# Four POOL subtractions of 512 columns in place of one of 2048, in a two-block transformer kernel

## The chip, the cores and the metric

The kernel runs on one core of a Trainium2 chip. Its time is the device time of one execution in microseconds (us). Five engines work side by side, each through its own queue of instructions, and are tied together by semaphores: PE (TensorE, matrix products), DVE (VectorE), ACT (ScalarE), POOL (GpSimd) and SP (SyncE, which here issues nearly all transfers).

## The reference

The input is 256 tokens of width 1024. The reference runs two blocks, one after the other. Cut to what matters here:

```
first_block:   adaptive RMS norm, convolution branch + attention branch, mixture of 32 experts (top 4), RMS norm
second_block:  x = layer_norm_2(x)
  layer 0:     mix = hybrid_mixer(x)           # attention + retention, gates
               x = layer_norm_2(ALPHA*x + mix)
               x = layer_norm_2(ALPHA*x + (silu(x @ w1) * (x @ w3)) @ w2)       # dense, width 2816
  layer 1:     mix = hybrid_mixer(x)
               x = layer_norm_2(ALPHA*x + mix)
               x = layer_norm_2(ALPHA*x + mixture of 8 experts (top 2))

layer_norm_2:  mu = mean(x); var = mean((x - mu)^2); (x - mu) * rsqrt(var + eps) * g + b
```

All of it is float32. Each weight matrix is read once from memory in pieces of 1 MB (128 partitions by 2048 columns).

## The kernel before, in words

The activations stand transposed, features on the partitions and tokens along the columns, as `X` (eight tiles of 128 features by 256 tokens; a "pair" is two of these, 512 columns).

For some of the second block's products (the projections qa, kva, ret and gg of both mixers, and ffn1 and ffn3 of the dense layer) the kernel doesn't multiply in float32. It writes weight and activation each as a sum of two parts in the faster type fp32r, a high part and a low part, and makes three passes: high weight by high x, low weight by high x, high weight by low x. There are 60 such pieces of weight, q = 0 to 59 in this profile's rows (19 of mixer 0, 22 of the dense layer, 19 of mixer 1). `split_dense` makes the two parts of piece q: ACT copies the raw weight into `WHI_D` (L379, which rounds it), then POOL subtracts that from the raw weight and writes `WLO_D` (L382). Both have room for four pieces. PE waits in `split_ready` for the low part of piece q, so for POOL; a raw slot is given back to SP for the next transfer by the same semaphore, `dense_lo`; and ACT may overwrite high part q only when PE has finished piece q - 4 (`lin_done`).

Nothing else orders POOL's work but its program: the pieces follow each other in the order of q; in the mixers two short masks of the retention decay (L565, L567) stand between a piece and the next. ACT splits as its own order allows: pieces 0 to 3 of each of the three stretches are split ahead, while a layer norm is still being computed, the others one by one as PE finishes pieces.

The layer norms before these stretches are what the prediction looks at. In each, DVE first takes a cheap estimate of the mean (SHIFT, L1650) from the columns. Then for each of four pairs it subtracts it (L2065 in the first norm, L2097 and L2100 in the others) and squares the result (`squared`, L1653). PE adds each pair and its squares over the partitions by products with a matrix of ones (`moments`, L727), for which it waits for DVE's square. In the first norm PE adds one more set of squares (L1000) between the third and the last pair. Then follow mean, variance and root on DVE and ACT (L1659 on), and the first product of the next stretch (`first_jobs`, L662). In the two later norms (after the mixer's w_out and after the dense layer) the pairs are mixed into the last products of the layer: L641 and L1235 are those products on PE, L2085 and L2201 DVE's adding of their results out of PSUM.

All of L2065, L2097, L2100 and L1653 read two operands from SBUF. L2085 and L2201 read one from SBUF and one from PSUM.

Of the kernel before, what the change touches and what calls it, by code (L numbers as in the profile page):

```python
# [20 lines left out]
F32 = mybir.dt.float32  # L21
F32R = mybir.dt.float32r
I32 = mybir.dt.int32
ALU = mybir.AluOpType
# [23 lines left out]
SLOT = 2048  # L48
# [90 lines left out]
def build_two_blocks(nc, A, out):  # L139
# [3 lines left out]
    with ctx:  # L143
        sems = {}

        def sem(name):
            if name not in sems:
                sems[name] = ctx.enter_context(nc.semaphore(name))
            return sems[name]
# [52 lines left out]
        def slot(n):  # L202
            r = n % RING if n < N_A else (n - N_A) % RING2
            return W[:, r * SLOT:(r + 1) * SLOT], r
# [162 lines left out]
        def split_dense(eng, q):  # L367

            n, _ = split_slots[q]
            raw, r = slot(n)
            if q >= SPLIT_N:
                eng.wait_ge(sem("lin_done"), split_slots[q - SPLIT_N][1])
            hi, lo = WHI_D[:, q % SPLIT_N, :], WLO_D[:, q % SPLIT_N, :]
            if eng is nc.scalar:
                eng.wait_ge(sem(f"arrived{r}"), arrive[n][1])
                eng.activation(hi, raw, ACT.Copy).then_inc(sem("dense_hi"), 1)  # L379
            else:  # L380
                eng.wait_ge(sem("dense_hi"), q + 1)
                eng.tensor_tensor(lo, raw, hi.bitcast(F32), ALU.subtract).then_inc(sem("dense_lo"), 1)  # L382

        def ring1(s):

# [127 lines left out]
        def _(pool):  # L513
# [42 lines left out]
            def mixer2(l):  # L556
                q0 = 41 * l
                for q in range(q0, q0 + 11):
                    split_dense(pool, q)
                for h in range(HEADS):  # L560
                    n = l * HEADS + h
                    pool.wait_ge(sem("decay_exp"), n + 1)
                    dec = DEC[:, h % 2, :]

                    ch.link(pool.affine_select(out=dec[:, 0:P], in_=dec[:, 0:P], compare_op=ALU.is_ge, fill=0.0,  # L565
                                               base=0, pattern=[[1, P]], channel_multiplier=-1))
                    pool.affine_select(out=dec[:, 3 * P:], in_=dec[:, 3 * P:], compare_op=ALU.is_gt, fill=0.0,  # L567
                                       base=0, pattern=[[-1, P]], channel_multiplier=1)\
                        .then_inc(sem("decay_masked"), 1)
                    split_dense(pool, q0 + 11 + h)  # L570

                pool.wait_ge(sem("ret_weighted"), HEADS * (l + 1))
                ch.link(pool.memset(SPREAD, 0.0))
                spread = SPREAD.rearrange("p k (g c) -> p k g c", g=2)
                for half in range(2):
                    i = pool.affine_select(out=spread[:, :, half, :], in_=spread[:, :, half, :], compare_op=ALU.not_equal,
                                           fill=1.0, base=-half, pattern=[[-2, KT], [0, HD]], channel_multiplier=1)
                i.then_inc(sem("pool_tables"), 1)
# [8 lines left out]
            for q in range(19, 41):  # L587
                split_dense(pool, q)
# [1671 lines left out]
```

## Time and profile before

| | |
|---|---|
| median of three runs | 2513.7 us (2511.43 to 2516.62) |
| the profiled execution's own time | 2516.26 us |
| its span, first to last instruction | 2514.5 us |
| PE busy | 2351.5 us, 94% |
| DVE busy | 724.7 us, 29% |
| ACT busy | 587.0 us, 23% |
| POOL busy | 298.9 us, 12% |
| mean granted TensorE clock | 0.966 |

A time of the table is that of a whole execution; the rows further down give the start of an instruction or a group of them in us from the start of the span, and how long it took. Busy time of DVE and POOL contains any time in which an instruction has been started and can't go on. The granted clock is a share of 2.4 GHz: 1.00 is that level, 0.50 is 1.2 GHz.

### The profile page before, as it was taken

Reading aid. Unit: us, or ns where it says so; the run is one execution under the profiler, and the core shown is the slowest. Engines: PE = TensorE matmul, PEld = TensorE weight load, DVE = VectorE, ACT = ScalarE, POOL = GpSimd, SP = SyncE. Lnnn points to the kernel's source line nnn. Section 1 sums busy time; section 2 is a strip of 40 time slices with the busy share of each in tenths; the row PEclk is TensorE's granted clock in tenths of the full one; section 3 lists DMA queues with packets and bytes.
Section 4 is the critical chain, followed back from the end, with each engine's and each line's share of the span. In section 5 each row is a group of like instructions: output and inputs, shape, how many; then the busy total and the mean of one; then the engine's idle time right before and its main releaser. Section 6 shows DMA issues by size and latency. Waiting matters only on the chain.

```text
span 2514.5 us, 35242 instructions
## 1 busy us (share of the span) xinstructions
PE 2351.5 (94%) x13516; PEld 1499.8 (60%) x13517; DVE 724.7 (29%) x1360; ACT 587.0 (23%) x865; POOL 298.9 (12%) x129
## 2 busy tenths in 40 slices
PE   3999879999999999999988999999899979999997
PEld 2887744444444444444447887899798874445444
DVE  5854222232222222222243324100313341111113
ACT  1033011121121111121233741430257011111111
POOL 1000000000000000000005532580265000000000
PEclk9999979999999999999998999999999979999998
DMA  9952449999999999989973423553543357799751
GB/s 374 363 176 86 117 166 417 418 418 417 418 418 418 418 418 417 417 339 418 418 306 116 135 68 117 168 185 117 168 137 107 110 225 276 290 407 402 278 231 62
DMA packets 226327, 688.60 MB, mean 274 GB/s; under 512 B 31338, under 2 KB 120242, under 8 KB 190418
## 3 DMA queue, kind: packets, MB, share of 16 engines
q1 hardware_dynamic: 221776, 685.82, 71.1%
q10 hardware_dynamic: 4482, 1.81, 0.3%
q8 instruction: 50, 0.82, 0.1%
q14 instruction: 19, 0.16, 0.0%
HBM read 686.53 MB, written 1.05 MB: 273 GB/s over the span
## 4 chain that ended last, share of the span: by engine, by line
PE 71%; DMA 11%; SPq 10%; DVE 5%; issue 2%; ACT 1%; ACTq 1%; DVEq 0%
PE PS L939 15%; PE PS L630 11%; PE PS L641 11%; DMA RAW<-in_w_exp_in 9%; SPq L434 6%; PE PS L1050 6%; PE PS L903 4%; PE PS L1061 3%; PE PS L1235 3%; SPq L456 2%; PE PS L922 2%; PE PS L1014 1%; PE PS L685 1%; PE PS L727 1%; PE PS L662 1%
## 5 line engine op out<-in xcount | busy, mean ns | idle before, releaser
L939 PE MATMUL PS<-RAW,Z 128*64 128x512 f32 x3168 | 715.5, 598 | 24.4 <-DMA RAW<-in_w_exp_in 23.6
L939 PEld LDWEIGHTS PS<-RAW,Z 128*64 128x64 f32 x3168 | 214.3, 137 | 456.3 <-issue 377.8
L382 POOL TENSOR_TENSOR WLO_D<-W,WHI_D 128x2048 fp32r<-128x2048 f32 x60 | 275.9, 4603 | 1321.7 <-ACT WHI_D L379 1321.7
L1050 PE MATMUL PS<-W,Z 128*64 128x384 f32 (+1 forms) x1408 | 216.0, 464 | 7.0 <-DMA W<-in_moe_w 5.8
L641 PE MATMUL PS<-Z,W 128*128 128x256 f32 x768 | 174.2, 388 | 2.2 <-DVE Z L1815 1.5
L1050 PEld LDWEIGHTS PS<-W,Z 128*64 128x64 f32 x1408 | 99.9, 138 | 124.2 <-issue 66.7
L641 PEld LDWEIGHTS PS<-Z,W 128*128 128x128 f32 x768 | 149.4, 195 | 26.0 <-DVE Z L1815 1.9
L379 ACT ACTIVATE WHI_D<-W 128x2048 fp32r<-128x2048 f32 x60 | 114.4, 1906 | 167.6 <-DMA W<-in_w_in 92.5
L903 PE MATMUL PS<-Z 128*128 128x64 f32 x1088 | 128.6, 278 | 3.1 <-DVE Z L1922 3.1
L903 PEld LDWEIGHTS PS<-Z 128*128 128x128 f32 x1088 | 127.4, 196 | 3.8 <-DVE Z L1907 3.8
L641 PE MATMUL PS<-H,W 128*128 128x256 f32 x512 | 118.3, 393 | 5.7 <-DVE H L1641 4.7
L1938 DVE TENSOR_TENSOR Z<-Z,PS 128x1024 f32<-128x1024 f32 x66 | 80.4, 1218 | 125.9 <-PE PS L922 125.9
L641 PEld LDWEIGHTS PS<-H,W 128*128 128x128 f32 x512 | 100.0, 197 | 21.3 <-DVE H L1641 4.8
L630 PE MATMUL PS<-XHI,WHI_D 128*128 128x256 f32 x784 | 112.0, 285 | 0.0
L630 PE MATMUL PS<-XHI,WLO_D 128*128 128x256 f32 x784 | 110.0, 283 | 0.0
L630 PE MATMUL PS<-XLO,WHI_D 128*128 128x256 f32 x784 | 110.0, 283 | 0.0
L1061 PE MATMUL PS<-W,Z 128*64 128x512 f32 x484 | 108.7, 597 | 0.0
L1450 ACT ACTIVATE Z<-PS 128x512 f32<-128x512 f32 x33 | 19.7, 597 | 367.6 <-PE PS L939 367.6
L630 PEld LDWEIGHTS PS<-XHI,WHI_D 128*128 128x128 f32 x784 | 100.6, 191 | 7.2 <-issue 7.2
L1965 DVE COPY Z<-PS 128x512 f32<-128x512 f32 x33 | 22.8, 692 | 280.5 <-PE PS L939 280.5
L630 PEld LDWEIGHTS PS<-XLO,WHI_D 128*128 128x128 f32 x784 | 101.1, 192 | 0.0
L630 PEld LDWEIGHTS PS<-XHI,WLO_D 128*128 128x128 f32 x784 | 101.1, 192 | 0.0
(376 smaller groups left out, 2410.6 us busy)
## 6 DMA issues: line engine op xcount, KB each, us to landing
RAW<-in_w_exp_in SPq DMA_DIRECT2D x256, 1024.0 KB, 19.3
RAW<-in_w_exp_out SPq DMA_DIRECT2D x128, 1024.0 KB, 21.8
W<-in_moe_w SPq DMA_DIRECT2D x128, 704.0 KB, 15.1
W<-in_w_in SPq DMA_DIRECT2D x52, 1024.0 KB, 5.7
W<-in_moe_w SPq DMA_DIRECT2D x40, 1024.0 KB, 14.4
W<-in_ffn_w SPq DMA_DIRECT2D x33, 1024.0 KB, 5.2
W<-in_w_ada SPq DMA_DIRECT2D x24, 1024.0 KB, 13.8
W<-in_w_out SPq DMA_DIRECT2D x12, 1024.0 KB, 4.9
```

Source lines behind the costliest of these rows:

```text
L379: eng.activation(hi, raw, ACT.Copy).then_inc(sem("dense_hi"), 1)
L382: eng.tensor_tensor(lo, raw, hi.bitcast(F32), ALU.subtract).then_inc(sem("dense_lo"), 1)
L434: sp.dma_start(dst, src).then_inc(sem(f"raw{s}"), 16)
L456: sp.dma_start(first2(s)[:, 1408 * i:1408 * (i + 1)], w[0, bass.ds(e, 1), s * P:(s + 1) * P, :].rearrange("a p n -> p (a n)"))\
L630: mm = pe.matmul(ps(job % 2, T, c0=j * T), w[:, k, c:c + P], xp[:, k, :], start=(i == k == 0), stop=(i == 2 and k == KT - 1))
L641: mm = pe.matmul(ps(job % 2, T, c0=j * T), w[:, k, c:c + P], x[:, k, :], start=(k == 0), stop=(k == nk - 1))
L903: mm = pe.matmul(ps(2, HALF, c0=k * HALF), HT[:, a, k * P:(k + 1) * P], PICK[:, a, 0:HALF], start=(a == 0), stop=(a == 1))
L939: mm = pe.matmul(ps(bank, 512, 64 * h, 64 * h + 64), x, w[:, c:c + 512], start=first, stop=final, skip_group_check=True)
L1050: mm = pe.matmul(ps(2 * i + b, n, 64 * h, 64 * h + 64), X1[:, s, :], first2(s)[:, c:c + n], start=(s == 0), stop=(s == 7), skip_group_chec ...
L1061: mm = pe.matmul(ps(2, 512, 64 * h, 64 * h + 64), x, second2(j)[:, c:c + 512], start=(i == j == 0), stop=(j == 5), skip_group_check=True)
L1235: mm = pe.matmul(ps(j // 2, T, c0=(j % 2) * T), w[:, i, j * P:(j + 1) * P], Z[:, k * T:(k + 1) * T], start=(k == 0 and j % 2 == 0), stop=( ...
L1938: dve.tensor_tensor(o, o, PS[:, 6:8, :].rearrange("p h (k t) -> p h k t", k=2), ALU.add)\
```

## The change

The low part of a piece is made by four POOL instructions of 512 columns in place of one of 2048. The bytes read and written are the same. The semaphore is raised by the fourth alone, so PE, ACT and SP are told at the same point of POOL's program as before. Nothing else is edited.

```
             else:
                 eng.wait_ge(sem("dense_hi"), q + 1)
-                eng.tensor_tensor(lo, raw, hi.bitcast(F32), ALU.subtract).then_inc(sem("dense_lo"), 1)
+                for c in range(0, SLOT, 512):
+                    i = eng.tensor_tensor(lo[:, c:c + 512], raw[:, c:c + 512], hi[:, c:c + 512].bitcast(F32), ALU.subtract)
+                i.then_inc(sem("dense_lo"), 1)
```

POOL's program where the second block begins, before. The iota of the first block is followed by pieces 0 to 10; the waits of each are given.

```order
L582 IOTA Z 128x256 [waits moe_scratch_free]
L382 TENSOR_TENSOR WLO_D<-W,WHI_D 128x2048 [waits dense_hi] x4
L382 TENSOR_TENSOR WLO_D<-W,WHI_D 128x2048 [waits dense_hi,lin_done] x7
L565 AFFINE_SELECT W<-W 128x128 [waits decay_exp]
L567 AFFINE_SELECT W<-W 128x128 [waits pool_step]
```

The same place now (pieces 0 and 1, then 4 and the masks; lines stand two or less further down the file):

```order
L584 IOTA Z 128x256 [waits moe_scratch_free]
L383 TENSOR_TENSOR WLO_D<-W,WHI_D 128x512 [waits dense_hi]
L383 TENSOR_TENSOR WLO_D<-W,WHI_D 128x512 x3
...
L383 TENSOR_TENSOR WLO_D<-W,WHI_D 128x512 [waits dense_hi,lin_done]
L383 TENSOR_TENSOR WLO_D<-W,WHI_D 128x512 x3
L567 AFFINE_SELECT W<-W 128x128 [waits decay_exp]
L569 AFFINE_SELECT W<-W 128x128 [waits pool_step]
```

The order of pieces and masks is kept. Within a piece the first instruction waits and the three behind it wait for nothing.

The second place is where POOL leaves mixer 0 for the dense layer, before (the spread table of the retention norm, then pieces 19 to 51):

```order
L573 MEMSET W 16x1024 [waits ret_weighted]
L576 AFFINE_SELECT W<-W 16x8x64 [waits pool_step]
L576 AFFINE_SELECT W<-W 16x8x64
L382 TENSOR_TENSOR WLO_D<-W,WHI_D 128x2048 [waits dense_hi,lin_done] x33
L565 AFFINE_SELECT W<-W 128x128 [waits decay_exp]
```

And now (the two last rows stand 33 times):

```order
L575 MEMSET W 16x1024 [waits ret_weighted]
L578 AFFINE_SELECT W<-W 16x8x64 [waits pool_step]
L578 AFFINE_SELECT W<-W 16x8x64
L383 TENSOR_TENSOR WLO_D<-W,WHI_D 128x512 [waits dense_hi,lin_done]
L383 TENSOR_TENSOR WLO_D<-W,WHI_D 128x512 x3
```

33 instructions became 132 there; over the program 60 became 240. The other engines' programs are the same as before.

## Rows read from the trace of the kernel before

**Rows 1.** The page's costliest groups: busy us, mean ns, idle before and releaser.
```profile
L382 POOL TENSOR_TENSOR WLO_D<-W,WHI_D 128x2048 fp32r<-128x2048 f32 x60 | 275.9, 4603 | 1321.7 <-ACT WHI_D L379 1321.7
```

**Rows 2.** PE's waits in the whole program: us in total, times, longest.
```profile
PE PS L727 <- DVE H L1653: 10.0, 4, 4.7
```

**Rows 3.** Timeline of DVE, first norm: start us, us, instruction.
```profile
1316.87 2.37 DVE L2065 TENSOR_TENSOR Z<-Z,SQ 128x512 f32<-128x512 f32 x1
1319.28 4.94 DVE L1653 TENSOR_TENSOR Z<-Z 128x512 f32<-128x512 f32 x1
1324.14 4.98 DVE L2065 TENSOR_TENSOR Z<-Z,SQ 128x512 f32<-128x512 f32 x1
1329.16 0.69 DVE L1653 TENSOR_TENSOR Z<-Z 128x512 f32<-128x512 f32 x1
```

**Rows 4.** Timeline of POOL, first norm (pieces 0, 1 and 2).
```profile
1314.17 4.52 POOL L382 TENSOR_TENSOR WLO_D<-W,WHI_D 128x2048 fp32r<-128x2048 f32 x1 [1007.05 <-ACT WHI_D L379]
1319.15 9.42 POOL L382 TENSOR_TENSOR WLO_D<-W,WHI_D 128x2048 fp32r<-128x2048 f32 x2 [0.47 <-ACT WHI_D L379]
```

**Rows 5.** Timeline of PE, first norm.
```profile
1324.27 3.78 PE L727 MATMUL PS<-Z,ONES 128*128 128x256 f32 x8 [7.90 <-DVE Z L1653]
1329.91 6.77 PE L727 MATMUL PS<-Z,ONES 128*128 128x256 f32 x16 [1.85 <-DVE Z L1653]
1336.51 3.62 PE L1000 MATMUL PS<-H,ONES 128*128 128x256 f32 x16
```

**Rows 6.** Windows: length, busy PE, PEld, DVE, ACT, POOL, granted clock, DMA, GB/s.
```profile
1329.90:1336.50 6.60, 6.59 (x16) 5.30 (x17) 2.54 (x4) 0.00 (x0) 0.00 (x0) 0.53 0.48 155
```

**Rows 7.** Timeline of DVE, second norm (after w_out of mixer 0).
```profile
1556.93 4.29 DVE L2097 TENSOR_TENSOR X<-X,SQ 128x512 f32<-128x512 f32 x1
...
1561.87 6.32 DVE L2100 SCALAR_TENSOR_TENSOR X<-X,SQ 128x512 f32<-128x512 f32 x3
```

**Rows 8.** Timeline of POOL, second and third norm (pieces 20, 21, 43, 44).
```profile
1556.15 4.52 POOL L382 TENSOR_TENSOR WLO_D<-W,WHI_D 128x2048 fp32r<-128x2048 f32 x1 [2.54 <-ACT WHI_D L379]
1563.09 4.55 POOL L382 TENSOR_TENSOR WLO_D<-W,WHI_D 128x2048 fp32r<-128x2048 f32 x1 [2.41 <-ACT WHI_D L379]
...
1789.73 4.52 POOL L382 TENSOR_TENSOR WLO_D<-W,WHI_D 128x2048 fp32r<-128x2048 f32 x1 [1.14 <-ACT WHI_D L379]
1798.35 5.03 POOL L382 TENSOR_TENSOR WLO_D<-W,WHI_D 128x2048 fp32r<-128x2048 f32 x1 [4.10 <-ACT WHI_D L379]
```

**Rows 9.** Timeline of PE, second norm.
```profile
1556.20 7.07 PE L641 MATMUL PS<-Z,W 128*128 128x256 f32 x32
...
1569.69 2.07 PE L727 MATMUL PS<-X,ONES 128*128 128x256 f32 x4 [4.69 <-DVE H L1653]
...
1573.26 7.96 PE L641 MATMUL PS<-Z,W 128*128 128x256 f32 x32
```

**Rows 10.** Timeline of DVE, third norm (after the dense layer).
```profile
1792.38 2.41 DVE L2097 TENSOR_TENSOR X<-X,SQ 128x512 f32<-128x512 f32 x1
...
1799.65 4.28 DVE L1653 TENSOR_TENSOR H<-X 128x512 f32<-128x512 f32 x1
```

**Rows 11.** Timeline of PE, third norm (third pair and fourth pair).
```profile
1803.99 2.07 PE L727 MATMUL PS<-X,ONES 128*128 128x256 f32 x4 [2.92 <-DVE H L1653]
...
1807.36 1.03 PE L727 MATMUL PS<-X,ONES 128*128 128x256 f32 x4
```

**Rows 12.** POOL's shortest kind of instruction: one column.
```profile
L540 POOL IOTA IOTAP<- 128x1 f32 x1 | 0.1, 137 | 0.1
```

**Rows 13.** Timeline of POOL: pieces 23 to 26, and 40, the dense layer's last.
```profile
1604.57 18.39 POOL L382 TENSOR_TENSOR WLO_D<-W,WHI_D 128x2048 fp32r<-128x2048 f32 x4 [29.06 <-ACT WHI_D L379]
...
1698.16 4.62 POOL L382 TENSOR_TENSOR WLO_D<-W,WHI_D 128x2048 fp32r<-128x2048 f32 x1 [1.13 <-ACT WHI_D L379]
```

**Rows 14.** Timeline of PE: first matrix products of pieces 23 and 40.
```profile
1615.27 1.12 PE L630 MATMUL PS<-XHI,WHI_D 128*128 128x256 f32 x8
...
1713.19 1.12 PE L630 MATMUL PS<-XHI,WHI_D 128*128 128x256 f32 x8
```

## The prediction, made before the changed kernel had run

> **What bounds the kernel now.** I read the page first: PE is busy 94% of the span, POOL 12%, in 60 instructions of 4.60 us each [rows 1]. By that POOL is no bound, and a change of its instructions could be worth nothing. The next view is who waits for whom, PE alone: it never waits for POOL. But it waits 10.0 us in four places for a square that DVE makes in the layer norms [rows 2], and in the first norm 7.90 and 1.85 us more [rows 5]. Third I read DVE's timeline at these waits, and that is where the change comes in. A subtraction or square of 512 columns takes DVE 0.69 us, yet three in a row end after 2.37, 4.94 and 4.98 us [rows 3]. POOL's timeline says why: its pieces run from 1314.17 to 1318.69 and, two of them, from 1319.15 to 1328.57 [rows 4]. The first long DVE instruction ends at 1319.24, 0.55 after POOL's piece; the third ends at 1329.12, again 0.55 after the end of a piece. In the second norm L2097 ends at 1561.22, and the piece at 1560.67: 0.55 [rows 7, 8]. In the third L1653 ends at 1803.93, the piece at 1803.38: 0.55 [rows 8, 10]. So a DVE instruction with both operands in SBUF stands still until the POOL instruction that runs has ended, and then needs 0.55 us. It holds the other way round as well: piece 44, begun at 1798.35 beside such a DVE instruction, takes 5.03 in place of 4.52 us [rows 8].
>
> The Trainium skill says the same ("SBUF — State Buffer", section on the two separate sides): a DVE instruction with two SBUF inputs and a GpSimd instruction that reads SBUF lock each other out for a whole instruction and don't share bandwidth. The trace agrees, by the four ends 0.55 us apart. Were it a sharing of bandwidth, cutting the instruction would bring nothing.
>
> Fourth I asked whether DVE gets its turn between two POOL instructions when POOL has the next one at hand. The middle of [rows 4] is the one case: pieces 1 and 2 take 9.42 us together, and within that L1653 ends at 1324.22 [rows 3], 0.55 after 1323.67, where piece 1 must have ended. Piece 2 then needs 4.35 us more (1328.57 less 1324.22). So they take turns.
>
> **What four short instructions cost on POOL.** No row shows such an instruction. From below: 4.52/4 = 1.13 us. From above: a POOL instruction for a single column takes 0.14 us [rows 12]; taken as pure start-up and added to 4.60/4 it makes 1.29. I take 1.20, between them. A piece is then 4.8 us (4.5 to 5.2) in place of 4.6.
>
> The Trainium skill gives figures for this operation ("GPSIMD Engine Reference", section on elementwise work): 2.6 cycles per element at 1.2 GHz and 4497 ns for 2048 columns. That leaves 60 ns for start-up and would make 1.17 us each, an estimate from that page; the sum would be the same. No run shows the split yet.
>
> Does this price reach PE? PE takes a new piece each 5.76 us in the dense layer ((1713.19 - 1615.27)/17 [rows 14]), POOL is through with piece 40 at 1702.78 [rows 13] and PE wants it at 1713.19: 10.4 us of cover, and POOL keeps up as long as a piece takes under 5.76 us. In the mixers the cadence is no faster. So 0 us, and still 0 at 1.29.
>
> **What it gives on DVE.** Turns: after a POOL instruction DVE needs 0.55 us; the next POOL instruction then needs its own time less 0.17 (4.52 less 4.35), so 1.03. A turn costs 1.58 us (1.51 to 1.67) where it was 4.90. I go through the three norms with that.
>
> *First norm.* DVE asks at 1316.87. POOL's quarters end at 1315.37, 1316.57, 1317.77, so DVE's first ends at 1318.3 and the following at steps of 1.58: the second (pair one ready) at 1319.9, the fourth (pair two) 1323.1, the sixth (pair three) 1326.2, the eighth 1329.4. POOL has work all along, since seven quarters do and twelve are to be made. PE starts pair one at 1319.9 and not at 1324.27 [rows 5]. Its products go at the lower level there, granted clock 0.53 from 1329.9 to 1336.5 [rows 6], 0.42 us each (6.77/16), 3.4 us a pair. So PE ends pair one at 1323.3, two at 1326.7, three at 1330.1, nearly without a gap, where before it idled between pairs. L1000 then starts at 1330.1 in place of 1336.51: 6.4 us. If the clock comes back one pair earlier (L1000's products take 0.22 us at the full level: 3.62/16), pair three takes 1.7 and it is 8.1 us. The worst: the clock stays low to the end of L1000 and the last pair; 24 products at 0.42 in place of 0.22 cost 4.8 us, and 1.6 are left. I take 7.0 (1.6 to 8.1).
>
> *Second norm.* DVE asks at 1556.93, the first quarter of piece 20 ends at 1557.35, and DVE's five instructions end at 1557.9, 1559.5, 1561.1, 1562.6 and, since piece 21 comes only at 1563.09, 1563.3. L2085 reads PSUM: 1564.0. The square of the next pair waits for one quarter and ends about 1565.0; PE has worked until then (the products of the first pair end about 1564.9) and does not wait 4.69 us [rows 9]. What follows ran at a lower clock after that wait: four products 2.07 us and the next 32 in 7.96 us, where the same take 1.03 and 7.07 [rows 9], and the other four of the pair cost about 0.9 more as well: 2.8 us. Full gain 7.5. If one more turn comes in the way, 1.6 less. If three turns do and the clock falls all the same, 2.5 are left. I take 6.0 (2.5 to 7.5).
>
> *Third norm.* The wait of 2.92 us [rows 11] and the slow products behind it (1803.99 to 1807.36 for eight that take 1.73 at full clock: 1.6 more). DVE's first instruction there, 2.41 us long, waits for piece 43 and was hardly on the path. Its second, which ran free, may meet the last quarter. With quarters DVE has pair three ready near 1800.5 in place of 1803.93; PE comes to it at 1800.6 and to the fourth pair at 1802.4 instead of 1807.36. That is 5.0; if pair two, which ran free before piece 44, now meets a quarter, 3.8. Only the wait shortened by two thirds and the clock still low: 1.9. I take 4.2 (1.9 to 5.0).
>
> Sum: 7.0 + 6.0 + 4.2 = 17.2 us (ends 6.0 and 20.6). The second mixer's last norm has no splits beside it, so nothing. In the mixers' attention DVE's 512-column instructions read PSUM and are not held. A gain in these norms moves everything behind it: PE works without such waits from each norm to the next, and the transfers there are issued as PE frees slots. The profiled execution took 2516.3 us, its span and 1.8 around it, so 2499.1 by its own time; it lies 2.6 above the median of the runs. Against the median, 2513.7 - 17.2 = 2496.5.
>
> **The rivals.**
> *No turn between quarters.* The three behind the first wait for no semaphore. POOL's queue may have them all under way before DVE asks, and DVE waits for four as it did for one. For it: pieces 23 to 26 ran in 18.39 us, 4.60 each, without a gap [rows 13], so POOL starts the next at once. Against it: pieces 1 and 2 also followed each other with the high part long made, and DVE came between. The semaphore wait between them is what is missing now. Time: gain 0, five long waits each longer by up to 0.3 us, 2514 to 2515. The Trainium skill's rule in "SBUF — State Buffer", on who interferes with whom, is that the order of issue decides who blocks; it doesn't say who is first between two queued instructions. Chance 0.11.
>
> *Turns, but PE's clock doesn't follow.* DVE's waits shrink but with one or two turns more than I count, and PE's products stay as slow as before. For it: after a wait of 2.92 us the clock fell, so one of 2 us could do it too. Gain about 4.4 (pair one earlier in the first norm) + 2.5 + 1.9 = 8.8, so 2504.9. Chance 0.30.
>
> *POOL becomes the bound.* If a quarter had a start-up far above 0.14 us, POOL would fall behind. Piece 23 starts at 1604.57 and PE wants piece 40 at 1713.19 [rows 13, 14], 18 pieces in 108.6 us: from 6.03 us a piece, 1.51 a quarter, PE waits in the dense layer, 18 x (c - 6.03). To lose the 17.2 us there c must be 7.0, a quarter 1.75 us; at 2.0 us a quarter it is 35 less 17, so 18 slower: 2532. Against it: 1.75 would be 0.6 of start-up where the shortest POOL instruction as a whole takes 0.14. Chance 0.03.
>
> *It doesn't do what it says.* No: 240 instructions of 512 columns stand in the program.
>
> **How the numbers follow.** The forecast of 2496.5 has 0.56, with its own range 2492 to 2501. Two in ten left out: the range goes from 2491 up to 2508, past the second rival. This kernel's runs differ by 0.1 to 0.2%, so 0.2%, 5 us, is about what can be told from no change. Faster by that: the forecast and nearly all of the second rival, 0.85. Within: the first rival and the rest, 0.12. Slower: 0.03.
>
> **What the profile after would show.** POOL's group: x240 at 1.13 to 1.29 us. DVE's L2065, L1653, L2097 and L2100: no instruction over about 1.8 us. PE's wait before the first L727 about 3.5 us and not 7.9; L1000 starts 14 to 16 us after POOL's first piece in place of 22; no wait of 4.7 us in the second norm. Behind the norms the timelines only shift. The forecast is wrong if DVE instructions of over 4 us remain (first rival), if they are short but L727 still comes at 0.42 to 0.47 us a product after the waits (second), or if PE waits for WLO_D at all (third).

## The result, and the profile after

The changed kernel takes 2493.6 us (median of four runs, 2493.1 to 2494.3) where the kernel before takes 2513.4 us (median of four): a ratio of 0.9924, interval 0.9911 to 0.9938. 19.7 us were gained; 17.2 were forecast. The profiled execution took 2493.8 us, with a span of 2492.1.

I read the views in the order of the prediction. POOL's group on the page, to be compared with [rows 1]:

```profile
L383 POOL TENSOR_TENSOR WLO_D<-W,WHI_D 128x512 fp32r<-128x512 f32 x240 | 308.8, 1322 | 1277.8 <-ACT WHI_D L379 1277.8
```

The same work keeps POOL busy for 33 us longer. The mean of 1322 ns is a little over the 1.29 us that the prediction gave as the upper end: a quarter that shares its time with DVE shows up to 1.76 us, and one that follows another starts 0.03 to 0.05 us before the end of the one ahead. From start to start, undisturbed quarters are 1.22 to 1.27 us apart. Then PE's waits for a square of DVE, which were 10.0 us for `H` [rows 2] and 9.75 for `Z` [rows 5]:

```profile
PE PS L729 <- DVE H L1655: 4.8, 3, 2.0
...
PE PS L729 <- DVE Z L1655: 3.7, 2, 2.9
```

So 11.3 us of PE's waiting went, and yet 19.7 us were gained. The timelines show where the rest came from. First norm, DVE (start, duration, instruction), against [rows 3]:

```profile
1313.49 0.69 DVE L2067 TENSOR_TENSOR Z<-Z,SQ 128x512 f32<-128x512 f32 x1
1314.22 1.65 DVE L1655 TENSOR_TENSOR Z<-Z 128x512 f32<-128x512 f32 x1
1315.79 1.76 DVE L2067 TENSOR_TENSOR Z<-Z,SQ 128x512 f32<-128x512 f32 x1
1317.59 1.64 DVE L1655 TENSOR_TENSOR Z<-Z 128x512 f32<-128x512 f32 x1
```

POOL beside it, pieces 0 to 2 in twelve instructions, against [rows 4]:

```profile
1311.10 18.40 POOL L383 TENSOR_TENSOR WLO_D<-W,WHI_D 128x512 fp32r<-128x512 f32 x12 [1006.94 <-ACT WHI_D L379]
```

And PE, against [rows 5]:

```profile
1315.92 5.96 PE L729 MATMUL PS<-Z,ONES 128*128 128x256 f32 x16 [2.92 <-DVE Z L1655]
1322.63 1.99 PE L729 MATMUL PS<-Z,ONES 128*128 128x256 f32 x8 [0.74 <-DVE Z L1655]
1324.46 3.62 PE L1002 MATMUL PS<-H,ONES 128*128 128x256 f32 x16
```

DVE's ends are 1.68 us apart (1317.55 to 1319.23). That is the turn: one POOL instruction, one DVE instruction. The first L2067 took 0.69 us, since a quarter ended (at 1313.61) just after DVE had asked. PE's first wait is 2.92 and not 7.90 us, and 16 products take 5.96 us where they took 6.77, the last eight 1.99. The windows of the same stretch say why (length, busy PE, PEld, DVE, ACT, POOL, granted clock, DMA, GB/s):

```profile
1315.90:1319.30 3.40, 3.38 (x8) 2.55 (x9) 3.37 (x3) 3.40 (x6) 3.40 (x3) 0.50 0.31 68
1319.30:1321.80 2.50, 2.50 (x9) 1.91 (x8) 2.47 (x2) 0.59 (x1) 2.50 (x2) 0.76 0.95 334
```

The clock leaves 1.2 GHz during the second pair; in [rows 6] it was still at 0.53 in the third. PE is then ahead of DVE: it waits 0.74 us for the third square. L1002 starts 11.4 us after DVE's first step of the norm (L1652 at 1313.04). Before it was 20.1. After POOL's first piece it starts 13.4 us (1324.46 less 1311.10), where the prediction looked for 14 to 16.

Second norm, DVE, against [rows 7], and PE, against [rows 9]:

```profile
1544.84 0.95 DVE L2099 TENSOR_TENSOR X<-X,SQ 128x512 f32<-128x512 f32 x1
1545.82 1.64 DVE L1655 TENSOR_TENSOR H<-X 128x512 f32<-128x512 f32 x1
1547.38 5.24 DVE L2102 SCALAR_TENSOR_TENSOR X<-X,SQ 128x512 f32<-128x512 f32 x3
```
```profile
1554.35 1.13 PE L729 MATMUL PS<-X,ONES 128*128 128x256 f32 x4 [1.45 <-DVE H L1655]
...
1556.18 7.07 PE L643 MATMUL PS<-Z,W 128*128 128x256 f32 x32
```

The wait is 1.45 in place of 4.69 us, and the products behind it run at full clock: 1.13 in place of 2.07 and 7.07 in place of 7.96. Third norm, DVE and PE, against [rows 10, 11]:

```profile
1780.16 1.41 DVE L1655 TENSOR_TENSOR H<-X 128x512 f32<-128x512 f32 x1
...
1782.20 1.05 DVE L1655 TENSOR_TENSOR H<-X 128x512 f32<-128x512 f32 x1
```
```profile
1781.62 1.13 PE L729 MATMUL PS<-X,ONES 128*128 128x256 f32 x4 [1.33 <-DVE H L1655]
```

The wait has moved: the second pair's square, free before, now meets a quarter (1.41), and the third pair's no longer stands for 4.28 (1.05).

Of the prediction's other signs, no DVE instruction of the four lines takes over 1.77 us, and PE never waits for a low part.

For all runs I cut the span at the same places. "Norm" is from the start of SHIFT on DVE (first norm) or of its sum on PE (second, third) to the first product of `first_jobs`; what lies between is "mixer 0", "dense", "mixer 1". Worked out from the timelines, us:

| run | norm 1 | mixer 0 | norm 2 | dense | norm 3 | mixer 1 |
|---|---|---|---|---|---|---|
| before | 30.82 | 208.11 | 34.19 | 201.26 | 23.32 | 206.05 |
| four of 512 (the change) | 22.14 | 208.06 | 28.33 | 200.79 | 19.57 | 205.86 |
| e1: all but the norms' pieces in four | 29.67 | 206.75 | 34.23 | 201.18 | 23.22 | 206.05 |
| e2: two of 1024 | 27.62 | 205.86 | 28.43 | 200.51 | 22.89 | 206.49 |
| e3: eight of 256 | 21.14 | 208.18 | 26.61 | 200.12 | 19.55 | 207.94 |
| e4: sixteen of 128 | 27.09 | 214.44 | 30.82 | 213.03 | 24.30 | 215.04 |
| e5: nine pieces, eight of 256 | 20.95 | 208.06 | 26.60 | 200.06 | 18.94 | 206.51 |
| e6: nine pieces, sixteen of 128 | 27.03 | 206.27 | 30.32 | 201.24 | 24.31 | 208.00 |
| e7: as e6, linked | 20.47 | 208.25 | 26.61 | 200.86 | 18.11 | 208.31 |
| e8: whole, five held | 22.78 | 206.60 | 26.61 | 199.97 | 18.47 | 205.88 |
| e9: four of 512, PE filled | 22.14 | 204.98 | 28.33 | 199.66 | 19.53 | 205.70 |
| e10: whole, PE filled in norm 2 | 30.64 | 208.09 | 31.33 | 201.00 | 23.08 | 205.97 |
| e11: pieces 0 to 2 in four | 22.15 | 207.96 | 33.93 | 201.28 | 23.26 | 206.12 |
| e12: e8 with PE filled | 21.42 | 205.52 | 26.61 | 199.67 | 18.50 | 205.66 |

The norms gained 8.68 + 5.86 + 3.75 = 18.3 us, the stretches between them 0.7. The spans differ by 22.4; the other 3.4 lie ahead of the first norm, which the profiled execution of before reached at 1316.41 and this one at 1313.04. 3.1 of them are there when POOL starts its first piece (1314.17 and 1311.10), so the change can't have made them. They are the spread between executions (the medians differ by 19.7), and differences up to about 2 us in the mixers are taken as such too: mixer 0 takes 206.27 us in e6, where its pieces are whole as before, against 208.11.

### The profile page after: what moved, and what is told of

It reads as the page before. It is cut to its first block, busy times and chain, and to the rows that moved or that the text cites. A ratio compares the mean times of both kernels' runs of the same rounds, so it can differ in the third digit from the quotient of the medians.

```text
span 2492.1 us, 35422 instructions
## 1 busy us (share of the span) xinstructions
PE 2343.3 (94%) x13516; PEld 1494.2 (60%) x13517; DVE 717.5 (29%) x1360; ACT 587.4 (24%) x865; POOL 331.8 (13%) x309
## 3 DMA queue, kind: packets, MB, share of 16 engines
HBM read 686.53 MB, written 1.05 MB: 276 GB/s over the span
## 4 chain that ended last, share of the span: by engine, by line
PE 74%; DMA 11%; SPq 8%; DVE 4%; issue 1%; ACT 1%; ACTq 1%; DVEq 0%
PE PS L941 16%; PE PS L632 11%; PE PS L643 11%; DMA RAW<-in_w_exp_in 9%; PE PS L1052 7%; SPq L436 6%; PE PS L1063 4%; PE PS L905 4%; PE PS L1237 3%; PE PS L924 2%; PE PS L1016 2%; PE PS L687 1%; PE PS L664 1%; PE PS L729 1%; PE PS L952 1%
## 5 line engine op out<-in xcount | busy, mean ns | idle before, releaser
L383 POOL TENSOR_TENSOR WLO_D<-W,WHI_D 128x512 fp32r<-128x512 f32 x240 | 308.8, 1322 | 1277.8 <-ACT WHI_D L379 1277.8
L1452 ACT ACTIVATE Z<-PS 128x512 f32<-128x512 f32 x33 | 19.7, 597 | 367.0 <-PE PS L941 367.0
```

The lines of the kernel that those rows point to most:

```text
L383: i = eng.tensor_tensor(lo[:, c:c + 512], raw[:, c:c + 512], hi[:, c:c + 512].bitcast(F32), ALU.subtract)
```

## The experiments

The theory: DVE instructions with both operands in SBUF and POOL's subtractions shut each other out for a whole instruction, a shorter instruction makes the wait shorter, and with it goes a time of low clock on PE. The rivals: the cut helps by itself wherever it is made; all is the wait, nothing the clock; POOL's start-up sets an end. Each ratio is to executions of the kernel before that were taken with the experiment (medians 2510.2 to 2510.7 us), so runs are compared by ratio.

**e1. Everything cut but the norms.**

```
+ w = SLOT if q in (0, 1, 2, 20, 21, 22, 42, 43, 44) else 512
```

> All pieces are cut into four except the nine that run beside a layer norm (0 to 2, 20 to 22, 42 to 44), which stay whole. Theory (turns between POOL and DVE in the three norms are the whole gain): no gain, 2512 to 2515 us; DVE's L2067, L1655 and L2102 again 4 to 5 us where they meet a piece. Rival (the cut helps by itself, in the 51 pieces beside the matrix products too): a good part of the 20 us stays, 2500 or less. POOL's group at 1.26 us for a cut instruction.

Ratio 1.0005 (0.9994 to 1.0016), 2513.4 us: no gain, and the interval leaves room for 1.5 us at most. PE's waits are those of before:

```profile
PE PS L730 <- DVE H L1656: 10.1, 4, 4.9
PE PS L730 <- DVE Z L1656: 10.1, 2, 8.2
```

204 of the 240 short instructions, beside the matrix products, are worth nothing that can be told. The gain lies in the nine pieces.

**e11. Only the first norm's pieces.** `w = 512 if q in (0, 1, 2) else SLOT`

> Only pieces 0, 1 and 2 cut into four, the rest whole. Theory (the norms' gains add up, each of its own): the first norm as with four everywhere, 22.1 us in place of 30.8, the second and third as before (34.2 and 23.3), gain 9 us, ratio 0.9965. Rival (an earlier start is given back in the next stretch, because transfers then pace it): a longer stretch between the norms, and a gain under 5.

Ratio 0.9966 (0.9952 to 0.9979), 8.5 us on 2511. Norm 1 takes 22.15 us as with all pieces cut, norms 2 and 3 stay near before, and the stretch behind is not longer. So the gain of this norm does not need the cuts in the others, and it is kept.

**e2. Two of 1024.** `w = 1024`

> Two instructions of 1024 columns for a piece. Theory: a DVE instruction waits for one POOL instruction, so a turn is the POOL instruction (2.33 us free) plus 0.44, 2.8 us, between the 4.9 of one and the 1.7 of four. First norm 3 us earlier (2 to 5), second 1, third 1.5: gain 5.5, 2508 us (2504 to 2510). Rival (the gain comes with any cut, since what matters is that POOL's queue lets DVE in at all): nearly the full 20 us, 2494 to 2497.

Ratio 0.9977 (0.9966 to 0.9988), 2505.2 us. DVE in the first norm:

```profile
1316.17 2.73 DVE L1656 TENSOR_TENSOR Z<-Z 128x512 f32<-128x512 f32 x1
1318.82 2.83 DVE L2068 TENSOR_TENSOR Z<-Z,SQ 128x512 f32<-128x512 f32 x1
```

A turn is 2.75 us (1318.90 to 1321.65), 2.8 expected. The price follows POOL's instruction, not the mere fact of a cut. By norms it came otherwise than I had split it: 3.2, 5.8 and 0.4, for 3, 1 and 1.5. Norm 2 turned on a near tie: DVE's third L2103 and the first half of piece 21 both start at 1554.05, and DVE gets through in 0.69 us. PE's wait is 1.55 us there and its clock stays up. The norms of this profile gained 9.4 us, more than the 5.8 of the ratio: the ten executions run from 2500.0 to 2507.7 us and the profiled one is the fastest of them, so such ties may fall otherwise in the rest. There is no profile of those.

**e3. Eight of 256.** `w = 256`

> Eight instructions of 256 columns. Start-up per further instruction 0.14 us ((4.94 - 4.52)/3), so 0.69 us each, 5.5 to 5.6 us a piece, under the 5.76 of PE's cadence: POOL still hidden. A turn is 0.70 + 0.44 = 1.14 us. Theory: the waits left in the norms (2.92, 1.45, 1.33 us) shrink by 1.1, 1.2 and 0.8, and 1 more in the first norm: gain 4 over four instructions, 2490 us (2488 to 2492). Rival (POOL's start-up grows faster, and PE waits for low parts): slower than four instructions, 2495 or more.

2492.1 us, ratio 0.9918 (0.9897 to 0.9938). 1.5 us better than four by the medians, within the intervals of both; 4 was expected. The norms gave 1.0, 1.7 and 0.0, and the second mixer took 2.1 more in this profile. PE's waits show no cause for it, so it counts as spread. The turn is 1.14 us as worked out. POOL stays hidden: 64 instructions in 44.53 us, 0.70 each, 5.6 a piece:

```profile
1344.71 44.53 POOL L384 TENSOR_TENSOR WLO_D<-W,WHI_D 128x256 fp32r<-128x256 f32 x64 [12.06 <-ACT WHI_D L379]
```

**e4. Sixteen of 128.** `w = 128`

> Sixteen instructions of 128 columns. By 0.14 us of start-up a piece is 4.6 + 15 x 0.14 = 6.7 us, over PE's 5.76: POOL sets the pace. PE waits for WLO_D in the dense layer, 18 x 6.7 - 108.6 = 12 us, and 1 us in each mixer; the finer turns give back 5. Theory: 2503 us (2498 to 2508), with PE waits on POOL in the profile. Rival (start-up is hidden in the instruction before, 0.08 or less each): a piece stays under 5.8, nothing is lost, 2488 to 2490.

2532.8 us, ratio 1.0083 (1.0064 to 1.0103): 21 to 22 us slower than before, not 7 faster. Three things are in it. POOL's pace is as worked out, 120.94 us for 288 instructions, 6.7 a piece, and the dense layer is 11.8 us longer, 12.1 by 18 x (6.7 - 6.03):

```profile
1599.69 120.94 POOL L384 TENSOR_TENSOR WLO_D<-W,WHI_D 128x128 fp32r<-128x128 f32 x288 [21.34 <-ACT WHI_D L379]
```

The mixers lose 6.3 and 9.0 us, not 1 each. I had left out the masks that stand behind the pieces in POOL's program; DVE gets them late in two places (its longest wait for L570, the second mask, is 5.3 us where it was 1.4) and PE waits for DVE. These waits of PE are 9.4 of the 15.3 us; for the rest PE's products ran longer (busy 1.0 and 5.9 us more). The waits, us in total, times, longest:

```profile
DVE W L2142 <- POOL W L570: 25.2, 16, 5.3
PE PS L1144 <- DVE W L2142: 9.4, 2, 5.6
PE PS L633 <- POOL WLO_D L384: 9.0, 13, 0.7
```

And the norms, in which finer turns should have given 5 us, lost two thirds of the gain (27.1, 30.8, 24.3 us: 6.1 of 18.3 are left). DVE in the first one, and POOL's batch beside it:

```profile
1313.47 0.69 DVE L2068 TENSOR_TENSOR Z<-Z,SQ 128x512 f32<-128x512 f32 x1
...
1318.39 0.94 DVE L2068 TENSOR_TENSOR Z<-Z,SQ 128x512 f32<-128x512 f32 x1
...
1327.88 6.97 DVE L1663 SCALAR_TENSOR_TENSOR SQ<-SQ 128x256 f32<-128x256 f32 x1
```
```profile
1311.07 23.50 POOL L384 TENSOR_TENSOR WLO_D<-W,WHI_D 128x128 fp32r<-128x128 f32 x48 [1007.05 <-ACT WHI_D L379]
```

The third row is the surprise of the study. At 1313.47 DVE comes to the running batch, behind six of its instructions, and gets its turn at once (0.69 us); as long as it then comes one instruction after the other, it keeps getting it (0.94 us). Eight us after the last of these it comes anew, and stands for 6.97 us until 1334.85; the batch had ended at 1334.57. When it came, POOL had put 18 instructions behind each other without DVE. In the other two norms it is the same: DVE stands for 5.3 and 5.7 us behind 23 and 20 such instructions. This is the prediction's first rival, no turn between short instructions, true in these places and not elsewhere in the same batches.

The runs with wider instructions do not settle whether the width decides or the number. The most that e3 had run undisturbed when DVE came, 12 instructions of 256 columns, took as long as e4's 20 (8.2 us), and DVE got in:

```profile
1763.35 12.95 POOL L384 TENSOR_TENSOR WLO_D<-W,WHI_D 128x256 fp32r<-128x256 f32 x16 [1.41 <-ACT WHI_D L379]
```
```profile
1771.55 0.76 DVE L2100 TENSOR_TENSOR X<-X,SQ 128x512 f32<-128x512 f32 x1
```

So it is not the time alone. 18 or more in a row were never met at 256.

**e6. Sixteen of 128, in the norms only.** So that POOL is not behind anywhere else.

```
+ w = 128 if q in (0, 1, 2, 20, 21, 22, 42, 43, 44) else SLOT
```

> The same nine pieces in sixteen of 128 columns. With all pieces cut so, three DVE instructions stood still for 5.3 to 7.0 us until POOL's whole batch had ended, beside others that got their turn after 0.2. Theory (POOL instructions this short leave DVE no opening when it comes new to a batch that is running): again DVE instructions of 4 us and more, and a gain of 10 to 16 us, smaller than with 256 columns. Rival (those three came from POOL being behind in the matrix stretches): no DVE instruction over 1.3 us, gain 22.

Ratio 0.9978 (0.9968 to 0.9987): 5.5 us of gain, less than the 10 to 16 that I gave the theory, but the DVE instructions are there, three again at the same places (7.10, 5.22, 5.68 us), behind the same 18, 23 and 20 undisturbed instructions. DVE in norms 1 and 2:

```profile
1327.48 7.10 DVE L1663 SCALAR_TENSOR_TENSOR SQ<-SQ 128x256 f32<-128x256 f32 x1
...
1565.14 5.22 DVE L1656 TENSOR_TENSOR H<-X 128x512 f32<-128x512 f32 x1
```

**e7. The same, each POOL instruction waiting for the one before.**

```
+                    if c + w < SLOT:
+                        cuts[0] += 1
+                        i.then_inc(sem("cut"), 1)
+                        eng.wait_ge(sem("cut"), cuts[0])
```

> As the run with nine pieces in sixteen of 128 columns, but each POOL instruction waits on a semaphore for the one before. If DVE is kept out because the next POOL instruction is already under way when one ends, it now always gets its turn: no DVE instruction over 1.3 us in the norms, at a price of 0.05 to 0.1 us per instruction on POOL, 1 to 1.5 us a piece, hidden. Gain 20 to 23 us. If the waits change nothing, DVE instructions of over 4 us are left as without them.

2489.9 us, ratio 0.9912 (0.9893 to 0.9931). The same two DVE instructions:

```profile
1326.66 0.42 DVE L1669 SCALAR_TENSOR_TENSOR SQ<-SQ 128x256 f32<-128x256 f32 x1
...
1559.63 0.98 DVE L1662 TENSOR_TENSOR H<-X 128x512 f32<-128x512 f32 x1
```

Same pieces, same columns, 16 us less: the shutting out needs POOL instructions that follow each other without a wait, for here DVE got in behind 14, 18 and 16 linked ones. The link also leaves POOL idle for about 0.08 us before each, and the run doesn't part that gap from the wait. The price of the link is 0.12 us, a little over the 0.05 to 0.1 expected: where DVE is away, linked instructions start 0.53 us apart (1320.05 to 1320.58) and unlinked ones 0.41. The first batch as a whole shows more, 0.66 each, since DVE's turns lie in it:

```profile
1309.93 25.77 POOL L386 TENSOR_TENSOR WLO_D<-W,WHI_D 128x128 fp32r<-128x128 f32 x39 [1006.52 <-ACT WHI_D L381]
```

A piece takes 8.5 us so (16 x 0.53), over 10 beside DVE's turns, which nine pieces can bear.

**e5. Eight of 256, in the norms only.** `w = 256 if q in (0, 1, 2, 20, 21, 22, 42, 43, 44) else SLOT`

> Only the nine pieces beside the norms are cut, into eight of 256 columns; the other 51 stay whole. Theory: the norms gain as with eight everywhere (first 9.7, second 7.6, third 3.8 us by the profiles), and the low parts beside matrix products are whole and early again: ratio to before about 0.9915, 21 us. Rival (cutting the other 51 also gives something): less than 17 us.

Ratio 0.9927 (0.9900 to 0.9954). One of its four executions took 4351 us and is left out of the ratio, which makes it a rough one. By the profile the norms gained 9.9, 7.6 and 4.4 us, 21.9 together, as expected; the ratio says 18 with 7 to either side, so the run agrees but adds little in the whole time.

**e8. No cut, five pieces held back.**

```
+                hold = {1: ("xw_shifted", 1), 2: ("normed", 8), 20: ("evac_dve", job_evac[lins["w_out0"].job0 + 2][1]),
+                        22: ("normed", 12), 44: ("normed", 16)}
+                if q in hold:
+                    eng.wait_ge(sem(hold[q][0]), hold[q][1])
```

> All pieces whole as before, but five are held back on POOL until DVE is past the part of a norm that they disturb: piece 1 until the last pair is shifted, 2, 22 and 44 until the norm is done, 20 until the third pair is added. Theory (the collision is all there is, not the length of an instruction): the waits of 7.9, 1.9, 4.7 and 2.9 us go without any cut; first norm 6 to 8.5 us, second 7, third 5, gain 18 to 20.5. Rival (held pieces come too late, and PE waits for WLO_D): a wait of PE on POOL in the profile, gain under 12.

2489.5 us, ratio 0.9908 (0.9888 to 0.9928), 21 to 23 us, a little more than expected. DVE's instructions in the second norm take 0.69 us, and POOL comes afterwards, released by DVE:

```profile
1545.21 0.69 DVE L2101 TENSOR_TENSOR X<-X,SQ 128x512 f32<-128x512 f32 x1
1545.93 0.69 DVE L1657 TENSOR_TENSOR H<-X 128x512 f32<-128x512 f32 x1
```
```profile
1552.44 9.42 POOL L386 TENSOR_TENSOR WLO_D<-W,WHI_D 128x2048 fp32r<-128x2048 f32 x2 [10.58 <-DVE X L2089]
```

PE waits for no low part. The length of the instruction was never the fault; the collision was. Norm 1 took 22.78 us, 0.64 more than in the changed kernel. Piece 0, still whole and not held, kept the first pair back: PE starts it 3.8 us after SHIFT, not 2.9. DVE had the second and third sooner, but PE could make no use of it, since its products ran at the low clock for longer (24 in 8.42 us):

```profile
1318.04 8.42 PE L731 MATMUL PS<-Z,ONES 128*128 128x256 f32 x24 [3.85 <-DVE Z L1657]
```

**e10. The clock's share, in norm 2.** The kernel before, with products of constants on PE during its wait.

```
                         moments(X, H, 0, True, False, 5, 4)
+                        for i in range(10 if l == 0 else 0):
+                            pe.matmul(ps(7, T), ONES[:, :], DIST[:, 0, :], start=True, stop=True)
                         moments(X, H, 1, False, False, 5, 4)
```

> The kernel before, POOL's pieces whole, with ten such products on PE between the first and the second pair of the second norm alone, where it waits 4.69 us for DVE. DVE comes no earlier. Theory (2.6 of the 5.9 us won in that norm are the clock, 3.2 the wait): from the first sum of that norm to the next first product 31.6 us in place of 34.2, with the products of the second pair at 0.22 us each. Rival (all of it is the wait): 34.2 as before. In the whole time 2.6 us are hardly to be told.

Norm 2 takes 31.33 us, 2.9 less, with DVE as late as ever. PE:

```profile
1560.77 4.48 PE L1219 MATMUL PS<-DIST,ONES 128*128 128x256 f32 x20
1565.40 1.13 PE L727 MATMUL PS<-X,ONES 128*128 128x256 f32 x4
```

The four products after the wait take 1.13 and not 2.07 us. So about half of what the change won in this norm (5.86) was clock. (The whole time, ratio 0.998 with 0.9971 to 0.9989, holds a gain of 2.9 us, at its lower end.)

**e9. The same filling ahead of first_jobs, on the changed kernel.**

```
 def first_jobs(lin):
+    for i in range(10):
+        pe.matmul(ps(7, T), ONES[:, :], DIST[:, 0, :], start=True, stop=True)
```

> The four-instruction kernel with ten further products (of constants, into a PSUM bank that nothing else uses then, never read) on PE ahead of each of the three first_jobs, where PE stands idle for 4.9 to 5.4 us. They change no output. Theory (the low clock behind an idle stretch is a cost by itself, on top of the wait): the products of first_jobs no longer start at 0.21 us a piece but at 0.12, each of the three stretches saves 1 to 2.5 us, 2486 to 2489 us. Rival (the clock falls and rises whatever PE did just before): no change, 2493 to 2495.

2487.9 us, ratio 0.9908 (0.9894 to 0.9921), as expected, though this interval and that of the changed kernel (0.9911 to 0.9938) overlap. In the profile mixer 0 is 3.1 us shorter, the dense layer 1.1, mixer 1 0.2; 3.1 is little over the spread between executions, and in e12 the same filling is worth 1.1, 0.3 and 0.2. The first stretch in windows, the changed kernel and then e9:

```profile
1335.10:1338.60 3.50, 3.42 (x16) 3.45 (x17) 2.72 (x5) 2.87 (x6) 0.00 (x0) 0.50 0.00 0
```
```profile
1333.90:1337.40 3.50, 3.26 (x23) 2.88 (x24) 2.71 (x5) 2.87 (x6) 0.00 (x0) 1.00 0.00 0
```

Granted clock 1.00 from the first product on, where it was 0.50. PE had stood idle for 5.37 us ahead of it in the changed kernel and for 1.06 in e9. The Trainium skill says this ("TensorE: Matmul & The Clock Gate", Part 1: the engine is slowed after a stretch without work), and the trace agrees, by 0.50 against 1.00.

**e12. Held pieces and filling together.**

> Pieces whole, five held back as in the run that held them, and the ten products ahead of each first_jobs. The two are independent: 4 to 6 us less than held pieces alone, ratio 0.989, 2483 to 2486 us, the fastest of the kernels here. If the products only shift the low clock elsewhere, no better than held pieces alone.

2487.6 us, ratio 0.9905 (0.9891 to 0.9919). No better than e9 or e8 beyond what the runs can tell, though its span in the profile is the shortest (2482.9). It and e9 are the fastest by their medians, 23 us under the kernel before. The expected 4 to 6 us over held pieces alone did not come. The stretches of the profile are 2.9 us shorter together, and 1.4 of these lie in norm 1, ahead of the filling, where the clock happened to come back sooner (24 products in 6.95 us where e8 has 8.42):

```profile
1315.13 6.95 PE L733 MATMUL PS<-Z,ONES 128*128 128x256 f32 x24 [3.95 <-DVE Z L1659]
```

## Why the prediction was right

**The mechanism** was right in each step. DVE needs its turn, gets it between two queued instructions, PE's wait shrinks, the clock follows. e1 shows that nothing else contributes over 1.5 us, e2 and e3 that the price is one POOL instruction plus 0.42 to 0.44 us, e8 that the collision and not the cut is what counts.

**The price on POOL.** 1.20 us per instruction was taken, 1.13 to 1.29 bounded. A quarter takes 1.24 us on its own (four in 4.94 us at 1537.36), beside busy engines 1.25 to 1.26. Each further instruction costs (4.94 - 4.52)/3 = 0.14 us. That is the duration of the one-column instruction [rows 12], which had been chosen as a bound; in part this is luck, since one-column memsets take less (0.10 to 0.11 us, L2250), so that it is not POOL's shortest, and since the bound added 0.14 to 4.60/4, which has a share of the start-up in it already. The 1.17 that the prediction estimated from the figures of the Trainium skill ("GPSIMD Engine Reference", section on elementwise work) is too low; the measurement decides. And it cost nothing: no wait for a low part in PE's list, as forecast.

**The turn.** 1.58 forecast, 1.68 measured.

**Norm 1.** 7.0 forecast, 8.68 measured, beyond its own upper end of 8.1. Two steps were mis-sized. PE's first wait was 2.92 us and not 3.5, because a quarter ended just after DVE had asked; that is a matter of phase. And I let the clock come back at the earliest with the third pair, since in [rows 6] it had needed two pairs. It came in the second (0.76 from 1319.3), so that DVE's third square and not PE set the start of the third pair. Why it came then is not shown. The gap between the pairs was gone, but that alone doesn't decide it: in e8, with no gap, the clock was back 6.1 us after PE's first product, in e12, whose edit in this norm is the same up to there, after 3.1. With the old gap of 1.85 us it came back late in the kernel before, and in e1 in time to make the 16 products behind the gap 5.31 us long, not 6.77:

```profile
1325.24 5.31 PE L730 MATMUL PS<-Z,ONES 128*128 128x256 f32 x16 [1.85 <-DVE Z L1656]
```

So e1, which is as the kernel before in this norm, has 29.67 and not 30.82 us. Taken from there the change won 7.5 us. Over 1 us of the 8.68 is thus luck of the two profiled executions.

**Norm 2.** 6.0 forecast, 5.86 measured. The full gain of 7.5 assumed that the third L2100 would run free. It did not, by very little: with turns of 1.68 us in place of 1.58 it comes at 1550.85, and piece 21, released by ACT's high part 6.84 us after the start of piece 20 (6.94 before), at 1550.81. One more turn was in the way. That is the branch "one more turn, 1.6 less". e3, e5, e7 and e8 have it without that turn: 26.6, 7.6 us less than before.

**Norm 3.** 4.2 forecast, 3.75 measured, the branch in which pair two meets a quarter (3.8).

**The sum** of 17.2 is 18.3 in the profile's norms and 19.7 by the runs (15.6 to 22.4 by the interval of the ratio). In the profile the first norm gave 1.7 us more than forecast, the others 0.1 and 0.4 less.

**The rivals.** "No turn between quarters" is false at 512 columns and true at 128 where many instructions had followed each other. It deserved its place, but I tied it to the wait between instructions alone; with three of four or seven of eight not waiting, DVE still gets in at 512 and 256. "The clock doesn't follow": false, it followed in all three norms. "POOL becomes the bound" needed a piece of 6.03 us in the dense layer; e4 with 6.7 a piece shows its size to be right (12.1 us by the formula, 11.8 measured), and that in the mixers the masks behind the pieces cost more than the pieces.

**Open.** What in POOL decides that DVE finds no opening. It was shut out behind 18 to 23 unlinked instructions of 128 columns and not behind 6 of them, nor behind 12 of 256 columns; whether the width or the number counts, and where between these it sets in, was not tried. That unlinked instructions reach for SBUF before the one ahead is through is only argued; e7 shows that a wait in between, with its gap, removes it. The clock's share in norm 1 was not measured by itself, nor what fixes the moment at which it comes back.

## What to carry to other kernels

An engine that is 12% busy and that nobody waits for can still set the time, if its long instructions shut out another engine on the path; look for the same instruction with two durations (0.69 and 4.9 us), and whose end the long one's end follows. Cut or, better, move the long instruction away from the serial stretches, and don't cut down to its start-up: with 0.14 us of it per instruction, 256 to 512 columns were enough here, and 128 made POOL the bound in the dense layer and, without waits between, lost turns. A wait that is removed on TensorE's path is worth more than its length where the clock falls with it: in norm 2 the change took 3.2 us off the wait and won 5.9.

## What the runs showed of the hardware that was not expected

- POOL instructions of 128 columns, 0.41 us apart and queued without waits, can keep a DVE instruction with two SBUF operands out until the batch ends (5.2 to 7.1 us, six times in two runs). Each time 18 to 23 of them had run without DVE between. Behind six of them DVE got in at once (0.69 us, twice), and DVE instructions that follow each other alternate with them (0.83 to 0.94 us). With a semaphore wait between POOL's instructions it never happened, behind up to 18.
- Such a wait costs 0.12 us per instruction on POOL, on top of the 0.14 of start-up.
- In one and the same stretch of products, from the low level, the granted clock came back 3.1 us after the first of them in e12 and 6.1 us in e8. A norm can differ by over 1 us by that alone.
- Ten products of constants on PE, 4.5 us in a gap of 5.4 us, keep the granted clock at 1.00 over it.
